# The even layer's input projection: the 32 sample rows multiplied unrounded, in four column groups and two halves

## What is computed

```
def _even_layer(x, mk, mv, C0, n0, m0, norm_g, w_in, b_if, ...):
    xn = _rms(x, norm_g)
    q, k, v, o, ig, fg, g_a, u, vb, g_b, xq, g_x = _split(xn @ w_in, EVEN_SPLITS)
    ...
    hA, C, n, m = _mlstm(heads(q), heads(k) * HEAD_DIM ** -0.5, heads(v), log_i, log_f, C0, n0, m0)
    yA = _rms(hA, h_g) * sigmoid(o) * silu(g_a)
    yB = _gmlp(u, _layernorm(vb, ln_g, ln_b), w_s, b_s) * silu(g_b)
    yX = _mem_attn(heads(xq), mk, mv, mem_qn) * silu(g_x)
    return x + concatenate([yA, yB, yX]) @ w_out
```

## Time and profile before

| | |
|---|---|
| median of 3 runs | 1839.22 us (1837.75 to 1840.47) |
| the profiled execution, its own time | 1835.88 us |
| span of its profile | 1834.3 us |
| PE busy | 1749.9 us, 95% of the span |
| PEld, DVE, ACT, POOL busy | 74%, 53%, 33%, 23% |
| 640 + 640 + 640 matmuls of layer 0's prompt units (L1282 to L1284) | 260.8 + 249.7 + 249.9 us |
| ten chunks' sample units (L1279, L1280) | 34.1 + 32.4 us |

### The profile page before, as it was taken

How to read it: one execution, slowest core, us unless ns; L and a number is a source line. 1 busy time by engine, 2 the same in 40 slices (tenths; PEclk the granted TensorE clock), 3 DMA queues, 4 the chain that set the end, 5 groups by cost and what they waited for, 6 DMA issues and landing times. The chain is left out here.

```text
span 1834.3 us, 26510 instructions
## 1 busy us (share of the span) xinstructions
PE 1749.9 (95%) x9413; PEld 1352.0 (74%) x9413; DVE 978.5 (53%) x2277; ACT 601.0 (33%) x1271; POOL 412.7 (23%) x643
## 2 busy tenths in 40 slices
PE   6999999999999999998999999999999679999999
PEld 5666788777888887886876567887777456777887
DVE  5422653233677655212541667888879665774111
ACT  3110332111122113101211346787735445553010
POOL 4301221100143452000341001211005455420000
PEclk9999999999999999999999999999999899999999
DMA  6433342545566467122222121334343775241231
GB/s 215 132 108 117 123 118 101 165 137 155 181 176 193 135 221 299 75 96 73 80 71 77 42 75 65 117 100 146 129 146 115 253 225 162 85 131 66 101 121 46
DMA packets 134765, 237.10 MB, mean 129 GB/s; under 512 B 28550, under 2 KB 61222, under 8 KB 134634
## 3 DMA queue, kind: packets, MB, share of 16 engines
q1 hardware_dynamic: 111066, 172.48, 29.0%
q0 software_dynamic: 17184, 55.85, 9.4%
q10 hardware_dynamic: 6384, 7.08, 1.1%
HBM read 169.12 MB, written 66.17 MB: 128 GB/s over the span
## 5 line engine op out<-in xcount | busy, mean ns | idle before, releaser
L1282 PE MATMUL ring_acc<-ring_w_hi,layer_xT_hi 128*128 128x512 f32 x640 | 260.8, 407 | 0.2 <-PE all_banks L1432 0.2
L1284 PE MATMUL ring_acc<-ring_w_hi,layer_xT_lo 128*128 128x512 f32 x640 | 249.9, 391 | 0.0
L1283 PE MATMUL ring_acc<-ring_w_lo,layer_xT_hi 128*128 128x512 f32 x640 | 249.7, 390 | 0.0
L2869 PE MATMUL front_acc<-front_w_hi,front_xT_hi 128*128 128x512 f32 x520 | 218.6, 420 | 10.5 <-DVE front_w_lo L3410 5.2
L2871 PE MATMUL front_acc<-front_w_hi,front_xT_lo 128*128 128x512 f32 x520 | 205.7, 396 | 0.0
L2870 PE MATMUL front_acc<-front_w_lo,front_xT_hi 128*128 128x512 f32 x520 | 205.5, 395 | 0.0
L1282 PEld LDWEIGHTS ring_acc<-ring_w_hi,layer_xT_hi 128*128 128x128 f32 x640 | 120.3, 188 | 29.5 <-issue 6.6
L1284 PEld LDWEIGHTS ring_acc<-ring_w_hi,layer_xT_lo 128*128 128x128 f32 x640 | 120.1, 188 | 26.1
L1283 PEld LDWEIGHTS ring_acc<-ring_w_lo,layer_xT_hi 128*128 128x128 f32 x640 | 120.4, 188 | 25.4 <-issue 2.6
L2869 PEld LDWEIGHTS front_acc<-front_w_hi,front_xT_hi 128*128 128x128 f32 x520 | 98.6, 190 | 43.3 <-issue 11.8
L3195 ACT ACTIVATE front_index_rows<-odd_bias,front_candidate 128x1024 bf16<-128x1024 f32 (+3 forms) x128 | 124.9, 981 | 9.0 <-DVEq L3559 5.1
(11 more groups left out here) (715 smaller groups left out, 3585.6 us busy)
## 6 DMA issues: line engine op xcount, KB each, us to landing
all_w<-in_w_even POOLq DMA_DIRECT2D x80, 256.0 KB, 3.8
h_even<-layer_st SPq DMA_DIRECT2D x79, 256.0 KB, 2.1
all_w<-in_w_odd POOLq DMA_DIRECT2D x61, 256.0 KB, 3.5
h_odd<-front_st SPq DMA_DIRECT2D x55, 256.0 KB, 2.1
layer_scratch<-h_even SPq DMA_DIRECT2D x46, 256.0 KB, 3.0
all_scratch<-in_w_mem SPq DMA_DIRECT2D x32, 256.0 KB, 3.6
all_scratch<-h_even SPq DMA_DIRECT2D x32, 256.0 KB, 3.6
all_scratch<-x SPq DMA_DIRECT2D x14, 512.0 KB, 3.9
```

The costliest lines, as they stand in the source:

```text
L1282: T.matmul(out[0:rows, :], xh[:, kk, to], wh[:, r, :], start=(kk == 0), stop=False)
L1283: T.matmul(out[0:rows, :], xh[:, kk, to], wl[:, r, :], start=False, stop=False)
L1284: ins = T.matmul(out[0:rows, :], xl[:, kk, to], wh[:, r, :], start=False, stop=(kk == KC - 1))
L2869: T.matmul(out[0:rows, :], xh[:, k, to], wh[:, r, :], start=(k == 0), stop=False, skip_group_check=True)
```

## The change

The sample tile no longer uses the split weights. Its transposed rows are kept once, unrounded (`x_smp`), and each raw slice is multiplied as it came from memory, in plain fp32. The 512 columns of a chunk are dealt to the four 32-column groups of the array: group g multiplies the 32 stationary columns by 128 columns of the slice and writes PSUM partitions 32g to 32g + 31. Since only four slices are in `raw` at a time, the eight slices are done in two halves: slices 0 to 3 of chunk c + 1 between the two halves of unit j = 3 of chunk c, into the other bank, which ACT at once copies to `hold` (128 x 128); slices 4 to 7 as unit j = 0 of chunk c + 1, and DVE adds `hold`. For chunk 0 both are done in unit 0. A stream step that `amid` puts inside a sample unit now comes after the whole of it. Results of the sample tile are 128 x 128 instead of 32 x 512. POOL's loads wait also for PE (`smp_mm`, `mm`), slices 4 to 7 of chunk 0 get buffers of their own, and the sample's gate columns are 8 plain matmuls instead of 24.

```
-        xh, xl, xl_smp = s.sb("xT_hi", [P, KC, TOK + SMP], F32R), s.sb("xT_lo", [P, KC, SEQ], F32R), ...
+        xh, xl = s.sb("xT_hi", [P, KC, SEQ], F32R), s.sb("xT_lo", [P, KC, SEQ], F32R)
+        x_smp, hold = s.sb("xT_smp", [P, KC, SMP]), s.sb("first_half", [P, P])
...
+        second = [X[:, 4096:4608], X[:, 4608:5120], S[:, 5632:6144], S[:, 6656:7168]]
+        raw_of = lambda n: second[n - RAW] if RAW <= n < KC else raw[n % RAW][:, :]
...
+        GATE_PARTS = (slice(SEQ, TOK), slice(0, 512), slice(512, SEQ))
+        HALF_AT = 3
...
             def load_w(n):
                 if n >= RAW:
                     pool.wait_ge(split_d, n - RAW + 1)
+                if n >= KC:
+                    was, kk = divmod(n - RAW if n >= KC + RAW else n - KC, KC)
+                    pool.wait_ge(*((smp_mm, was + 1) if kk < RAW else (mm, T1 * was + 1)))
...
+            def sample(chunk, part, out, start=True, stop=True):
+                for kk in range(RAW * part, RAW * part + RAW):
+                    n_w = KC * chunk + kk
+                    pe.wait_ge(w_in[n_w % RAW], 16 * (n_w // RAW + 1))
+                    for g in range(4):
+                        ins = T.matmul(out[32 * g:32 * g + SMP, 0:P], x_smp[:, kk, :], raw_of(n_w)[:, P * g:P * g + P],
+                                       start=(start and kk % RAW == 0), stop=(stop and kk % RAW == RAW - 1))
+                return ins
...
             def half(n, side):
...
-                    if chunk == 0:
-                        pe.wait_ge(xe, 2 * j + 2)
+                    if chunk == 0 and j:
+                        pe.wait_ge(xe, 2 * j)
+                    if j == HALF_AT + 1 and chunk + 1 < len(ORDER):
+                        pe.wait_ge(held, chunk + 1)
+                    if n == 0:
+                        pe.wait_ge(upper, RAW + 2)
+                        sample(0, 0, out, stop=False).then_inc(smp_mm, 1)
+                    if j == 0:
+                        sample(chunk, 1, out, start=(chunk > 0)).then_inc(mm, 1)
+                elif j == HALF_AT and chunk + 1 < len(ORDER):
+                    pe.wait_ge(*evacuated(n - 1))
+                    sample(chunk + 1, 0, psD[(n + 1) % 2]).then_inc(smp_mm, 1)
+                if j == 0:
+                    return
...
 (ACT, dense)
+                if j == HALF_AT and chunk + 1 < len(ORDER):
+                    if chunk:
+                        act.wait_ge(*evacuated(T1 * chunk))
+                    act.wait_ge(smp_mm, chunk + 2)
+                    A(hold[:, :], psD[(n + 1) % 2][:, 0:P], ACT.Copy, scale=1.0 if ORDER[chunk + 1][1] == COPY else 0.5).then_inc(held, 1)
...
 (DVE, dense)
+                if of_sample(n):
+                    dve.wait_ge(mm, n + 1)
+                    if chunk:
+                        dve.wait_ge(held, chunk)
+                    if kind(n) != COPY:
+                        V.scalar_tensor_tensor(acc, acc, 0.5, hold[:, :], ALU.mult, ALU.add).then_inc(whole, 1)
+                    elif chunk:
+                        dve.wait_ge(*stored_by(n - ST))
+                        V.tensor_tensor(y, acc, hold[:, :], ALU.add).then_inc(ev_v, 1)
+                    else:
+                        V.tensor_copy(y, acc).then_inc(ev_v, 1)
```

More of the change, by code:

```diff
@@ L1339, in gate_rows @@
                     if j == 0:
-                        pe.wait_ge(xe, 2 * T1)
+                        pe.wait_ge(xe, 2 * TILES)
                     if j == 2:
                         pe.wait_ge(gev, 1)
-                    low = xl_smp if j == 2 else xl[:, :, to]
-                    products(T, psB[0:36, 512 * (j % 2):512 * (j % 2) + to.stop - to.start],
-                             [((wif[:, 0, kk, :], wif[:, 1, kk, :]), (xh[:, kk, to], low[:, kk, :])) for kk in range(KC)]).then_inc(gmm, 1)
+                    out = psB[0:36, 512 * (j % 2):512 * (j % 2) + to.stop - to.start]
+                    if j == 0:
+                        for kk in range(KC):
+                            ins = T.matmul(out, wpad[:, kk, :], x_smp[:, kk, :], start=(kk == 0), stop=(kk == KC - 1))
+                    else:
+                        ins = products(T, out, [((wif[:, 0, kk, :], wif[:, 1, kk, :]), (xh[:, kk, to], xl[:, kk, to])) for kk in range(KC)])
+                    ins.then_inc(gmm, 1)
                     yield
@@ L1842, in slice_w @@
             def slice_w(n):
-                chunk, r, from_ = n // KC, n % RING, raw[n % RAW]
+                chunk, r, from_ = n // KC, n % RING, raw_of(n)
                 dve.wait_ge(w_in[n % RAW], 16 * (n // RAW + 1))
```

112 lines of the change are left out of this document (51 added, 61 removed).

## The result

| | before | changed |
|---|---|---|
| median of 5 runs | 1839.22 us (1836.49 to 1842.02) | 1847.17 us (1841.29 to 1849.18) |
| the profiled execution, own time / span | 1835.88 / 1834.3 us | 1841.29 / 1839.7 us |
| PE busy | 1749.9 us | 1738.4 us |
| first product of layer 0's next stage (L333) starts | 699.4 us | 704.6 us |

The ratio is 1.0041, 95% interval 1.0024 to 1.0059: slower by about 0.4%. Between the two profiled executions the difference is 5.4 us, and 5.2 of it lie in the changed layer's front: the next stage starts 5.2 us later, and from there on the two profiles are 1134.9 and 1135.1 us long. All ratios here are of undisturbed executions: one of `e3_moved` (3503 us) and one of `e5_one_place` (2901 us) are left out.

The account below looks back on a forecast made before the run. PE's own in-order list was taken to bound layer 0's front until PE must wait: -12.8 us won + 10.4 insertions + 8.6 clock = +6.2 on the 1839.2 us median, giving 1845.4 us, range 1835 to 1852.

Parts of the forecast that it names:

- fixed chains and a lowered clock: Main forecast: other engines' chains in chunks 6 to 8 stay put, new waits lower PE's clock; 1845.4 us, chance 0.53.
- chunks 1, 3, 4, 5 won: Unit 0 of these chunks: nothing behind shows a wait, so each wins the full 2.77 us, 11.1 us together.
- nine insertions: Other half unit inside unit 3 of chunks 0 to 8: 1.15 us each with entry and exit, 10.4 us spent.
- waits in chunks 6, 7, 8: Behind these sample units, PE's waits of 0.81, 0.91 and 1.54 us grow by 2.77 to 3.6, 3.7, 4.3.
- clock and rest of chunks 6, 7, 8: Clock falls behind the three new waits cost 2.3 us each, less 0.9 in chunk 7: 6.0 us together.
- clock at the start: Chunk 0: the array's rise to full clock may come later, into unit 1; 0 to 3 us, taken as 1.5.
- What stands behind each sample unit: After the ten sample units: time is won only where the next item is ready earlier; 12.8 us won in all.
- The clock: Layer 0's front: granted clock falls to 0.50 behind new long waits, 1.1 us in chunk 2; 8.6 us in all.
- POOL's extra waits end in units 0 and 3, five units before their slices are used: POOL's weight-slice loads, which now also wait for PE: costed at nothing.
- the signs named: Front's profile: PE busy about 17 us less, three waits of 3.5 to 4.5 us, chunks 1, 3, 4, 5 1.6 shorter.
- The parallel groups: Rival, half units: four groups fully parallel, 0.86 us instead of 1.02, saving 3.0 us, at most 1842.4; chance 0.06.
- The chains come forward: Rival, chunks 6 to 8: DVE's chain comes earlier, waits and clock falls go, 8.3 us more won, 1830; chance 0.12.

Follow-up runs that it names:

- e3_moved: Changed kernel with three PE stream steps of chunks 6, 7 and 8 placed 2.8 us later each; ratio to the kernel before 1.0014.
- e5_one_place: Changed kernel with both sample half units in unit 0, none in unit 3 (slices 4 to 7 multiplied twice); ratio to the kernel before 1.0032.
- e2_before_cut: Kernel before with 2 of the 16 matmuls of each sample unit, nothing put into unit 3; ratio to the kernel before 0.9982.
- e1_fill: The cover put back: changed kernel plus 16 unread matmuls of 384 columns in the sample units of chunks 6, 7, 8; ratio to the kernel before 1.0034.

## Why the prediction was right, and where its terms were off

The forecast was 1845.4 us, slower, by the case of fixed chains and a lowered clock; 1847.2 was measured, inside that case's own range. That the sum came within 2 us of the median is in part luck: the clock's terms were 4.7 us too dear in the first profile, the 3.0 us of chunk 4 were missing, and the two profiled executions differ by 5.4 us where the medians differ by 7.9. Term by term, first profile against before by the ends of units:

| step of the prediction | predicted, us | measured, us |
|---|---|---|
| chunks 1, 3, 4, 5 won | 4 x 2.77 | 2.6, 2.5, 2.5, 2.5 |
| chunk 2 won | 0.7 | 0.7 |
| chunk 9 won | 1.0 | 1.0 |
| chunks 0, 6, 7, 8 won | 0 | 0.3 in chunk 0; the three in the clock's row |
| nine insertions | 10.4 | 10.7 (1.21 to 1.25, chunk 5 0.87) |
| waits in chunks 6, 7, 8 | 3.6, 3.7, 4.3 | 3.5, 3.1, 4.0 |
| clock and rest of chunks 6, 7, 8 | 2.3, 1.4, 2.3 | 2.0, 0.5, 1.4 |
| clock in chunk 2 | 1.1 | 0 |
| clock at the start | 1.5 | 0 in the first profile, 2.0 in the second |
| chunk 4 | 0 | 3.0: 1.3 of waiting for cached keys, 1.7 of clock |

- **What stands behind each sample unit** held in chunks 7 and 8: the waits came at the named instructions, and the kernels with sample units of 0.4 to 3.8 us have the same 7.2 to 7.7 us in chunk 7. In chunk 6 the wait came at the named instruction too, but "none of it depends on how fast PE passes the sample unit" was too strong: in both kernels the four DMAs of L933 run beside loads of weight slices, which in the changed kernel start behind the sample unit. With the cover put back they ran before the loads, and DVE followed 4.2 us after their start instead of 6.2 (6.5 in the kernel before).
- **The clock** was right as a cause and mis-sized as a term: I took 2.3 us per fall from rows of 3.4 to 6.85 us; in both profiles of the changed kernel each fall in chunks 6 to 8 lasted 3.4 us, so cost 1.7. In other kernels some lasted 6.8. The trace of before had a shorter wait with a fall behind it, which the prediction passes over: 1.99 us in front of 699.40 (L333), with 0.50 from 700.40 to 703.80.
- **Chunk 4 was the step that failed**, and with it "POOL's extra waits end in units 0 and 3, five units before their slices are used", which was costed at nothing. PE came to the cached keys 3.5 us earlier than in the kernel before (333.62 against 337.10), but that alone makes no wait: `e2_before_cut` came at 331.56 and did not wait. SP started their DMA 5.4 us earlier too (326.39 against 331.82). The DMA took longer. In the kernel before, POOL started the four loads of the next weight slices one by one from 319.46 to 322.65, as DVE freed the buffers; in the changed kernel they wait for the sample unit and start together, right before the keys' DMAs:

```profile
324.98 2.12 POOL L1120 DMA_DIRECT2D all_w<-in_w_even  x4 [20.89 <-PE ring_acc L1282]
326.39 1.03 SPq L870 DMA_DIRECT2D layer_scratch<-in_cache_mem_k  x2
334.93 1.30 PE L1481 MATMUL all_banks<-all_ident,layer_scratch 128*128 128x128 f32 x5 [1.31 <-DMA layer_scratch<-in_cache_mem_k]
```

  The first two DMAs of the cached keys, with their median time from issue to landing, in the changed kernel, the kernel before and `e2_before_cut`:

```profile
layer_scratch<-in_cache_mem_k SPq DMA_DIRECT2D x2, 512.0 KB, 9.8
```

```profile
layer_scratch<-in_cache_mem_k SPq DMA_DIRECT2D x2, 512.0 KB, 4.4
```

```profile
layer_scratch<-in_cache_mem_k SPq DMA_DIRECT2D x2, 512.0 KB, 4.3
```

  The first of the two took 8.3 to 10.3 us in all ten profiles of kernels with the new tile, and 3.7 to 4.4 in the four with the old one. No run changed the loads alone, so that they are the cause is argued from these times.
- **PE busy** fell by 10.1 us in the stretch of the earlier trace rows (11.5 in the whole kernel), where 17 was predicted apart from the clock. A stretch at 0.50 counts as busy: four of them hold 13.6 us in which PE did about 6.8 us' worth of work, and 17 less 6.8 is 10. Of the signs named, chunks 1, 3 and 5 became 1.3, 1.2 and 1.7 us shorter (1.6 expected), chunk 4 1.8 us longer; the wait in chunk 7 was 3.1 us, under the 3.5 to 4.5 named.
- **The parallel groups.** I let the row of `state_terms` speak against the factor of four. The row was right for what it shows, 1.02 us for one run of 32 records among others; but of that only 0.87 us grow with the number of records, 0.027 us each against 0.107 on the whole array, 3.9 times as fast. The Trainium skill (TensorEngine Tiling (Array Packing), Overview, Theoretical Speedup) gives up to four; the doubled insertion agrees with it. It changed little here, since the ways in and out (0.36 us) take back what the products save.
- **The chains come forward** stayed a rival only: in no kernel with the old order did the step in chunk 7 come more than 0.5 us earlier, counted from the prompt unit before it. In chunk 6 it came 1.0 us earlier than in the kernel before in `e1_fill` alone, where the weight loads start late.

What stays open: whether the new sample tile with the best order is faster than the old one with it. The ends of the fronts say 1 to 2 us, the medians nothing. Whether weight loads that start one by one, or later, take chunk 4's wait away and bring chunk 6's chain forward was not tried. And why the clock falls behind 1.3 us of waiting in chunk 4 and not behind 1.8 in chunk 2 was not tried.

## What to carry to other kernels

In a list that an engine works in order, a shortened item buys nothing where the next one waits for a chain on another engine; look up, behind each place, when the next item's input was ready. Look also at which transfers of other engines the edit lets start at the same time: a wait of POOL that cost nothing by itself was followed by a DMA of twice the length on PE's path. Then give the steps behind the shortened item a later place in the list together with the edit: here the same 33 us of removed products were worth 3.3 us in the old order and 21 us in one with seven steps half a unit later, and the order alone was worth 5. By the ends of units most of it was won in chunks 0 to 5; in chunks 6 to 9 the order mainly stopped losses. A small detour in fp32 between rounded products has a fixed price (0.36 us here), so such insertions should be few and large.

## What was unexpected of the hardware

- The clock's falls depend on more than the length of the wait before them. Behind 1.3 us in chunk 4 it fell, as in all eight profiles with the new tile and the old place of the cached keys' step, where the wait was 1.3 to 2.5 us. Behind up to 1.8 us in chunk 2 it fell in none of those (behind 2.2 us there, in `e2_before_cut`, it did). Behind a wait of 2.0 us in front of L333 it fell in the kernel before and not in the changed one. And a wait of 3.5 us in chunk 6 was followed by 3.4 us at 0.50 in the changed kernel and by 6.8 us in `e5_one_place`.
- A wait that costs 4 us by itself cost up to 3.4 us more through the clock (chunk 6 of `e2_before_cut`, 6.8 us at 0.50 right behind it). Idle matmuls in the place of such waits made a stretch faster: 9 us of added work, 4.6 us less time, of which 1.4 come from a DMA chain that ended sooner.
- Two DMAs of 512 KB took 8.5 and 11.1 us to land beside four weight loads of 256 KB that had started within 1.6 us of each other around them (changed kernel, chunk 4); in the kernel before, where those loads had landed, 4.0 and 4.8.
